# Where tile 1's turns stand in the head of a stage: one move on TensorE's queue in a two-block transformer kernel

## The reference

```python
# first block, a layer l
x = x + einsum("bsc,cd->bsd", mixed, w_out[l])
h = rms_norm(x, ffn_norm_g[l])
u = causal_dwconv(einsum("bsd,df->bsf", h, ffn_w_in[l]), ...) + ffn_conv_b[l]
x = x + einsum("bsf,fd->bsd", silu(gate) * up, ffn_w_out[l])
# second block, a layer i
x = x + 0.5 * rms_norm_2(swiglu(rms_norm_2(x, g[0]), ...), g[1])
x = x + rms_norm_2(mixer(rms_norm_2(x, g[2])), g[3])
x = x + 0.5 * rms_norm_2(swiglu(rms_norm_2(x, g[4]), ...), g[5])
```

## Time and profile before

| what | value |
|---|---|
| median of 3 runs | 2595.43 us (2595.39 to 2599.72) |
| profiled execution, first to last instruction | 2589.7 us |
| what lies around it, against the median | 5.7 us |
| TensorE busy | 2560.5 us, 99% |
| VectorE busy | 1687.8 us, 65% |
| ScalarE busy | 1322.3 us, 51% |
| GpSimd busy | 158.0 us, 6% |
| read from memory | 456.37 MB, 177 GB/s |

### The profile page before, as it was taken

How to read it: one execution, slowest core, us unless ns; L and a number is a source line. 1 busy time by engine, 2 the same in 40 slices (tenths; PEclk the granted TensorE clock), 3 DMA queues, 4 the chain that set the end, 5 groups by cost and what they waited for, 6 DMA issues and landing times.

```text
span 2589.7 us, 43298 instructions
## 1 busy us (share of the span) xinstructions
PE 2560.5 (99%) x18489; PEld 2376.5 (92%) x18489; DVE 1687.8 (65%) x2365; ACT 1322.3 (51%) x1938; POOL 158.0 (6%) x228
## 2 busy tenths in 40 slices
PE   9999999999999999999999999999999999999998
PEld 8999898998998989989988998998899899897997
DVE  7778577885664766656556765656776566566663
ACT  7766376663543554444455444444554354355542
POOL 2110011000000000000011000002000000000000
PEclk9999999999999999999999999999999999999999
DMA  7267452764766546666665766756467566563863
GB/s 227 95 182 209 158 163 82 196 195 158 209 195 207 176 131 194 189 179 193 190 212 149 200 184 183 196 182 195 142 159 192 193 178 191 196 202 100 217 189 120
DMA packets 568313, 460.26 MB, mean 178 GB/s; under 512 B 10298, under 2 KB 529290, under 8 KB 568122
## 3 DMA queue, kind: packets, MB, share of 16 engines
q1 hardware_dynamic: 562615, 441.91, 58.0%
q0 software_dynamic: 4656, 15.30, 1.8%
q10 hardware_dynamic: 851, 0.28, 0.0%
HBM read 456.37 MB, written 1.10 MB: 177 GB/s over the span
## 4 chain that ended last, share of the span: by engine, by line
PE 90%; DVE 5%; ACT 3%; DMA 1%; issue 1%; POOL 0%; SPq 0%; DVEq 0%; POOLq 0%; ACTq 0%
PE ps L911 28%; PE ps L776 16%; PE ps L778 16%; PE ps L777 16%; PE ps L730 3%; PE ps L732 3%; PE ps L731 3%; DVE wlo L1899 1%; ACT h_hi L1315 1%; PE ps L653 1%; ACT prob L1315 1%; DVE h_lo L1961 1%; ACT whi L1315 1%; DMA raw<-in_w_in 1%; PE ps L1013 1%
## 5 line engine op out<-in xcount | busy, mean ns | idle before, releaser
L1899 DVE TENSOR_TENSOR wlo<-raw,whi 128x2048 fp32r<-128x2048 f32 (+1 forms) x419 | 957.4, 2287 | 495.4 <-ACT whi L1315 495.1
L1315 ACT ACTIVATE whi<-raw 128x2048 fp32r<-128x2048 f32 (+2 forms) x421 | 802.7, 1910 | 790.2 <-DMA raw<-in_ff_w_in 418.1
L776 PE MATMUL ps<-h_hi,whi 128*128 128x256 f32 x3584 | 1005.7, 281 | 0.0
L778 PE MATMUL ps<-h_hi,wlo 128*128 128x256 f32 x3584 | 1002.5, 280 | 0.0
L777 PE MATMUL ps<-h_lo,whi 128*128 128x256 f32 x3584 | 1001.8, 280 | 0.0
L776 PEld LDWEIGHTS ps<-h_hi,whi 128*128 128x128 f32 x3584 | 673.9, 188 | 5.0 <-issue 5.0
L778 PEld LDWEIGHTS ps<-h_hi,wlo 128*128 128x128 f32 x3584 | 674.4, 188 | 0.0
L777 PEld LDWEIGHTS ps<-h_lo,whi 128*128 128x128 f32 x3584 | 673.5, 188 | 0.0
L911 PE MATMUL ps<-whi,hid_lo 128*128 128x512 f32 x880 | 296.3, 396 | 0.0
L911 PE MATMUL ps<-whi,hid_hi 128*128 128x512 f32 x880 | 295.4, 394 | 0.0
L911 PE MATMUL ps<-wlo,hid_hi 128*128 128x512 f32 x880 | 294.6, 394 | 0.0
(11 more groups left out here) (315 smaller groups left out, 2142.8 us busy)
## 6 DMA issues: line engine op xcount, KB each, us to landing
raw<-in_ff_w_in SPq DMA_DIRECT2D x176, 1024.0 KB, 6.0
raw<-in_ff_w_out SPq DMA_DIRECT2D x88, 1024.0 KB, 4.9
raw<-in_ffn_w_in SPq DMA_DIRECT2D x44, 1024.0 KB, 6.1
raw<-in_a_w_qkv SPq DMA_DIRECT2D x24, 1024.0 KB, 5.2
raw<-in_ffn_w_out SPq DMA_DIRECT2D x22, 1024.0 KB, 4.9
raw<-in_w_in SPq DMA_DIRECT2D x18, 1024.0 KB, 6.1
raw<-in_c_w_qkv SPq DMA_DIRECT2D x12, 1024.0 KB, 5.3
raw<-in_w_out SPq DMA_DIRECT2D x8, 1024.0 KB, 4.9
```

What stands on the lines that cost most here:

```text
L776: e.matmul(out, hi, m.h_hi[:, k, :], start=(k == 0), stop=False)
L778: ins = e.matmul(out, lo, m.h_hi[:, k, :], start=False, stop=(k == KT - 1))
L1315: return self.nc.scalar.activation(*a, **k)
L1899: self.e.tensor_tensor(chunk_view(m.wlo[:, slot, :], c), chunk_view(m.raw[:, slot, :], c), chunk_view(m.whi[:, slot, :], c).bitcast(F32), ...
```

## The change

The step at which tile 1's turns are called becomes an argument. At scaled edges it stays what it was: chunk 1, before step 3. At all other edges, thirteen of them, it becomes chunk 0, before step 5, both in tile 0. So the turns stand behind five steps of the head there, and not behind eleven.

```diff
-    def tokens_tile(self, b, t, w=256, features=False, between=None, gates=False):
+    def tokens_tile(self, b, t, w=256, features=False, between=None, gates=False, place=3):
...
-            if between is not None and k == 3:
+            if between is not None and k == place:
                 between()
...
-    def head(self, turn, kind):
+    def head(self, turn, kind, turn_at):
...
-                self.tokens_tile(b, t, widths[b], features=(b == 0), between=turn if (t, b) == (0, HEAD - 1) else None, gates=gates)
+                self.tokens_tile(b, t, widths[b], features=(b == 0), between=turn if (t, b) == (0, turn_at[0]) else None,
+                                 gates=gates, place=turn_at[1])
...
-        self.head(lambda: self.turn_tile(1, scaled), after[0])
+        self.head(lambda: self.turn_tile(1, scaled), after[0], (HEAD - 1, 3) if scaled else (0, 5))
```

## The result

The changed kernel takes 2604.77 us (median of 5 runs, 2603.36 to 2606.24) against 2595.39 us before (5 runs on the same chip): ratio 1.0037, 95% interval 1.0026 to 1.0048. That is 9.4 us slower by the medians; the forecast was 10.9 us and 2606.3 us. The profiled execution's span grew from 2589.7 to 2601.2 us, by 11.5. In the runs on record a time lies 2.1 to 2.7 us above the span of its own execution; so of the 5.7 us between the profiled span and the median in the table of before, about 3.5 us are scatter between executions.

A forecast was written before the change was run, and what follows sets the result against it. TensorE, busy 99% of the span, was taken as the bound, so only its waits matter. 11.9 us lost less 0.95 gained gives 10.9 us, on the 2595.43 us median 2606.3 us; range 2602.0 to 2611.0.

The forecast's parts named there:

- weighted edge: Eleven of thirteen moved edges, whose residual goes through square, GpSimd power and two additions; 1.08 us lost each, 11.9 together.
- h_lo wait: TensorE's wait at tile 1's part for the low half of the next stage's features; 0.45 us an edge, to vanish.
- Bare edges: Two edges, ffn1 into mix1 and into swiglu, with only one addition; gain 0.5 and 0.45 us, together 0.95.
- second rival: Lost time is given back by shrinking later waits; all absorbed leaves 7.2 us, 2602.6; 7% part absorbed, 5% no change.
- first rival: TensorE works past the waiting turns, so thirteen edges gain their h_lo wait: 5.9 us faster, 2589.5 us; chance 3%.
- the rival: TensorE's clock falls after the idle at each weighted edge: 3.9 us an edge, 43 in all, near 2649; chance 2%.
- likeliest case: The forecast itself: eleven weighted edges lose, two bare edges gain, 2606.3 us; spans 2605.5 to 2609.7 by its bounds; 83%.

The follow-up runs named there:

- early_residual: The changed kernel, but tile 1 is added into x with tile 0's norm factor, without waiting for its own; ratio 1.0028 to the kernel before.
- changed_again: The changed kernel looked at once more, nothing altered; span 2603.9 us, one run.
- three_steps: Against the kernel before: turns at weighted edges behind three steps of the head, bare edges in their old place; ratio 1.0104.
- ten_steps_again: The kernel of ten_steps run once more, with more rounds; ratio 0.9977 to the kernel before.
- ten_steps: Against the kernel before: turns at weighted edges behind ten steps of the head, at bare edges behind five; ratio 0.9981.
- split_turns: Against the kernel before: at weighted edges left half's turns behind nine steps, right half's behind ten; bare edges behind five; ratio 0.9974.

## Why the prediction was right

- *The turns are reached 1.77 us into the head and then wait for x.* Right: two groups of four with 1.30 and 0.24 us of idle weight loads, as at the edge of the earlier trace rows. The total named L2007 is 17.9 us where I wrote "some 16": 16.9 are the eleven edges, the rest are short waits for x elsewhere.
- *The residual's path does not depend on the turns.* Right: 3.64 us before and after, and early_residual shows that moving it moves the loss by the same 0.57 us.
- *1.08 us lost at a weighted edge, from the 0.47 us between addition and resumption.* Measured 8.43 - 7.35 = 1.08; the 0.47 measured where tile 0's turns already had this wait holds for tile 1's.
- *The h_lo wait goes away inside that sum.* Right: 6.2 us became 1.0, all at the scaled edges and the start.
- *Bare edges gain 0.45 and 0.5.* Measured 0.46 and 0.57.
- *Nothing else pays or gives back.* 0.57 us of the rest differ between the two profiles, within what two executions of one kernel differ by (changed_again's rest is 2.8 us above the first's). The second rival would have needed several microseconds off the rest.
- *Matmuls do not pass a waiting turn.* Right; the first rival is out at all eleven edges.
- *The clock.* The clock stayed at 1.00 at all eleven edges, as forecast, but the reason was weak. The 1.46 us of idle in the earlier trace rows are two waits, 0.95 and 0.52 us, at the end of the fourth mixer, where the clock stayed up in all fourteen executions. A similar row of short waits, at the end of the differential-attention stage, ran at 0.83 in other executions, so one stretch at full clock proves little. What bears the forecast out came later: none of 33 edges with the 1.30 us wait, while turns two steps sooner (three_steps) make the clock fall at half the edges. The price that I gave the rival, 3.9 us an edge, was too high: a fall costs 1.4 to 1.6 us.

The sum of 10.9 us meets 10.93 us in the heads. That the median came only 1.5 us below the forecast is partly luck: the medians differ by 9.4 us with an interval of about 6.7 to 12.5, the rest differs between two executions of the changed kernel by 2.8 us, and the likeliest case's own range, 2605.5 to 2609.7, held only the bounds of the terms and not this scatter; the median lies 0.7 us below it.

## What to carry to other kernels

An instruction that waits blocks all that is behind it, so its best place on an in-order queue is the first at which its data are there, and both directions have a price: here 0.35 us for each step too early, and up to 0.45 us when what it feeds becomes late. A wait can cost more than its length: at 2.00 us the fall of the clock added 1.4 to 1.6 us at half the edges. Read the arrival time of the data for each kind of caller separately: one place for all edges was right for two of thirteen and wrong for eleven. Where the time of a whole execution scatters by more than the effect, sum the edited stretches in the trace, and look at the granted clock of the rest before believing a difference of spans.

## What was not expected of the hardware

After a wait of 2.00 us (weight loads) the granted clock fell to the lower level at 11 of 22 edges, for equal instructions and equal waits, and not at the same ones in two executions. The ends of two mixer stages show the same without any edit near them (0.83 or 1.00 over ten microseconds). The seven executions in which the clock fell at neither of these, nor at an edge, have rests of 2479.0 to 2481.9 us; the six in which it fell at one of these ends, 2481.9 to 2486.2.

Stages made of the same instructions take one of a few lengths: the ffn1 stage's rest was 180.82 us in most executions and 181.48 or 181.49 in others. The 0.66 us are no wait: in the first ffn1 stage the 960 products of lines 777 to 779 start over 113.12 us in ten_steps_again (154.07 to 267.19) and over 113.81 in ten_steps (153.87 to 267.68), the difference builds up evenly over them, and the granted clock is 1.00 in both. Why each takes 0.7 ns longer stays open.

Four transposes as a group of their own take 0.36 us (split_turns) where eight together take 0.79.
